# A streaming encoder layer on one core: the feed-forward down projection in two passes over all row blocks, one per half of the output columns

## The reference

```python
x = x + conv_glu_ffn(rms_norm(x, g_ffn), w_up, conv_ffn, b_conv_ffn, w_down)

def conv_glu_ffn(u, w_up, conv_ffn, b_conv_ffn, w_down):
    h = causal_dwconv(u @ w_up, conv_ffn) + b_conv_ffn      # D_FF = 5632, conv width 3
    return (jax.nn.silu(h[..., :D_FF]) * h[..., D_FF:]) @ w_down
```

## Time and profile before

| | |
|---|---|
| median of three runs | 1746.23 us |
| the profiled execution's own time | 1744.13 us |
| its span, first to last instruction | 1742.3 us |
| TensorE busy | 1736.8 us |
| VectorE busy | 1117.4 us |
| ScalarE busy | 938.1 us |
| read from and written to HBM | 326.83 MB, 2.10 MB |
| chunk loads, 512 KB each | 600 |

### The profile page before, as it was taken

The page is one execution under the profiler, slowest core; times in us unless marked ns, Lnnn a source line. Parts: engine busy times, 40 slices in busy tenths (PEclk is TensorE's granted clock), DMA queues, the critical chain, the costliest instruction groups (busy, mean ns, idle before and its releaser), DMA issues.

```text
span 1742.3 us, 26005 instructions
## 1 busy us (share of the span) xinstructions
PE 1736.8 (100%) x8742; PEld 1476.3 (85%) x8742; DVE 1117.4 (64%) x1555; ACT 938.1 (54%) x1273; POOL 9.9 (1%) x22
## 2 busy tenths in 40 slices
PE   9999999999999999999999999999999999999999
PEld 7888888888888888888888888888888888888887
DVE  6788876667855455545665666767777666755554
ACT  7765656667754444444654565555555555544443
POOL 0000000000000000000000000000000000000000
PEclk9999999999999999999999999999999999999999
DMA  8555554476655555556855446555555555655554
GB/s 324 190 172 173 173 171 157 169 166 166 177 184 194 187 193 192 192 188 230 294 183 188 149 159 193 193 193 193 192 185 189 191 187 190 191 193 193 193 193 156
DMA packets 91237, 330.79 MB, mean 190 GB/s; under 512 B 10256, under 2 KB 10512, under 8 KB 90160
## 3 DMA queue, kind: packets, MB, share of 16 engines
q1 hardware_dynamic: 89712, 321.96, 55.7%
q0 software_dynamic: 1472, 8.12, 2.8%
HBM read 326.83 MB, written 2.10 MB: 189 GB/s over the span
## 4 chain that ended last, share of the span: by engine, by line
PE 99%; DMA 0%; DVE 0%; SPq 0%; ACT 0%; issue 0%
PE ps L350 22%; PE ps L331 14%; PE ps L333 14%; PE ps L332 14%; PE ps L353 11%; PE ps L739 4%; PE ps L738 4%; PE ps L737 4%; PE ps L453 1%; PE ps L454 1%; PE ps L452 1%; PE ps L497 1%; PE ps L496 1%; PE ps L609 0%; PE ps L511 0%; PE ps L504 0%
## 5 line engine op out<-in xcount | busy, mean ns | idle before, releaser
L1309 DVE TENSOR_TENSOR w_lo<-w_raw,w_hi 128x1024 fp32r<-128x1024 f32 x598 | 729.4, 1224 | 573.3 <-ACT w_hi L785 572.4
L785 ACT ACTIVATE w_hi<-w_raw 128x1024 fp32r<-128x1024 f32 x598 | 629.0, 1058 | 647.8 <-PE ps L333 310.2
L350 PE MATMUL ps<-u,w_hi 128*128 128x512 f32 x1664 | 580.8, 395 | 0.0
L353 PE MATMUL ps<-u,w_lo 128*128 128x256 f32 x1664 | 461.8, 278 | 0.0
L350 PEld LDWEIGHTS ps<-u,w_hi 128*128 128x128 f32 x1664 | 312.1, 188 | 72.0
L353 PEld LDWEIGHTS ps<-u,w_lo 128*128 128x128 f32 x1664 | 312.7, 188 | 0.2
L331 PE MATMUL ps<-w_hi,u 128*128 128x512 f32 x608 | 240.9, 396 | 0.5 <-DVE w_lo L1341 0.5
L333 PE MATMUL ps<-w_hi,u 128*128 128x512 f32 x608 | 237.2, 390 | 0.0
L332 PE MATMUL ps<-w_lo,u 128*128 128x512 f32 x608 | 237.0, 390 | 0.0
L331 PEld LDWEIGHTS ps<-w_hi,u 128*128 128x128 f32 x608 | 114.4, 188 | 24.4 <-issue 1.1
L333 PEld LDWEIGHTS ps<-w_hi,u 128*128 128x128 f32 x608 | 114.2, 188 | 24.3
(11 more groups left out here) (344 smaller groups left out, 1917.5 us busy)
## 6 DMA issues: line engine op xcount, KB each, us to landing
w_raw<-in_stream SPq DMA_DIRECT2D x600, 512.0 KB, 3.4
x_tok<-in_x SPq DMA_DIRECT2D x2, 1024.0 KB, 8.4
mem_raw<-in_mem_by_feature POOLq DMA_DIRECT2D x2, 1024.0 KB, 9.0
x_tok<-in_x POOLq DMA_DIRECT2D x2, 1024.0 KB, 7.6
mem_tok<-in_mem POOLq DMA_DIRECT2D x2, 1024.0 KB, 14.8
out<-x_tok SPq DMA_DIRECT2D x8, 256.0 KB, 3.3
x_t<-in_x_t SPq DMA_DIRECT2D x7, 256.0 KB, 5.2
w_raw<-in_stream SPq DMA_DIRECT2D x4, 256.0 KB, 4.5
```

Of the source, the lines that this page charges most:

```text
L350: pe.matmul(ps[:, bank + m, :], w_hi[:, s, lo:lo + P], act[:, kc, :, :].rearrange("p h t -> p (h t)"), start=(kc == 0), stop=False)
L353: mm = pe.matmul(ps[:, bank + m, T:2 * T], w_lo[:, s, lo:lo + P], act[:, kc, 0, :], start=False, stop=(kc == KC - 1))
L785: act.activation(w_hi[:, s, :], w_raw[:, s, :], ACT.Copy).then_inc(hi_made, 1)
L1309: TTo(w_lo[:, s, :], w_raw[:, s, :], w_hi[:, s, :].bitcast(F32), ALU.subtract).then_inc(lo_made, 1)
```

## The change

- The 88 chunks of w_down come in another order: first the left 1024 columns for all 44 row blocks, then the right 1024 columns for all 44. TensorE goes over the row blocks twice. A pair of row blocks (`p`, 22 in all) goes with two chunks in each pass.
- Each pair is split once, in pass 0, and stays: the low parts in `h_lo`, in the place of `h_ff`; the high parts in three homes: `h_hi_a` for pairs 0 and 1, `h_hi_b` for pairs 2 to 13 (in the place of most of `u`, the up projection's input), `h_hi_c` for pairs 14 to 21 (in the place of ua, ub, xa, xb and on). `h_st` is gone. `stage` works on a pair (128 by 512) instead of a block (128 by 256); pairs 0 and 1 are staged where round 0 was.
- The loops are gone: all 88 chunks are written out on PE, ACT and DVE.
- PE waits in pass 0 for `h_low` of each pair before the pair's first chunk; ACT and DVE prepare chunks two pairs ahead (`down_split(n + 2)`) and stage pair n + 2 behind that.
- When pass 0 is over, DVE adds banks 0 to 3 in one instruction (128 by 2048) to the left half of `x_tok`, and SyncE's queue stores that half in two transfers of 512 KB behind the last chunk load. At the end PE goes over banks 4 to 7 with the last pair (6 matmuls each), and only these four are added and stored.
- In other parts of the kernel some semaphores are merged into one that counts through them (small_made, small_T, c_tok, mg_parts, norm_mv and so on); each wait is for the same event as before.

```diff
-DOWN_PER = 8
-DOWN_ITER = FC * 2 // DOWN_PER
+QN = FC // 2
...
-        STORES = [(bank, (bank % 4) // 2, (2 * (bank // 4) + bank % 2) * BLK) for bank in range(8)]
+        STORES = [(bank, (bank % 4) // 2, (2 * (bank // 4) + bank % 2) * BLK) for bank in range(4, 8)]
...
@@ SyncE @@
+            sp.wait_ge(sem("half_made"), 1)
+            for t in range(TT):
+                sp.dma_start(out[t * P:(t + 1) * P, 0:1024], x_tok[:, t, 0:1024]).then_inc(sem("stored"), 16)
...
@@ TensorE @@
+            def down_products(s, p, k, t, n, bank, first=False, last=False):
+                rows, at = slice(t * P, (t + 1) * P), slice(n * BLK, (n + 1) * BLK)
+                return three(ps[:, bank, :], h_high(p, k)[:, rows], h_lo[:, 2 * p + k, rows],
+                             w_hi[:, s, at], w_lo[:, s, at], first, last)
+            def down_plain(j, p):
+                g = G_DOWN + 2 * (QN * j + p)
+                for k in range(2):
+                    pe.wait_ge(lo_made, g + k + 1)
                     for t in range(TT):
                         for n in range(2):
+                            mm = down_products((g + k) % SLOTS, p, k, t, n, 4 * j + 2 * t + n, first=(p == 0 and k == 0),
+                                               last=(j == 0 and p == QN - 1 and k == 1))
                     mm.then_inc(w_used, 1)
+            for j in range(2):
+                for p in range(QN):
+                    if j == 0:
+                        if p == 0:
+                            pe.wait_ge(sem("up_sum"), 2 * UP_ITER - 1)
+                        pe.wait_ge(sem("h_low"), p + 1)
+                    elif p == 0:
+                        pe.wait_ge(sem("up_sum"), 2 * UP_ITER)
+                    if j == 0 or p < QN - 1:
+                        down_plain(j, p)
+            for k in range(2):
+                pe.wait_ge(lo_made, G_END - 1 + k)
+            for bank, t, at in STORES:
+                for k in range(2):
+                    mm = down_products((G_END - 2 + k) % SLOTS, QN - 1, k, t, bank % 2, bank, last=(k == 1))
                 mm.then_inc(sem("bank_done"), 1)
...
@@ ScalarE @@
+            def stage(p):
+                act.activation(h_high_pair(p), h_pair(h_ff, p), ACT.Copy).then_inc(sem("h_high"), 1)
+            def down_split(n):
+                g = G_DOWN + 2 * n
+                s = g % SLOTS
+                for k in range(2):
+                    act.wait_ge(landed[s + k], Pos(g + k).landed(0))
+                    act.wait_ge(w_used, g + k - SLOTS + 1)
+                    act.activation(w_hi[:, s + k, :], w_raw[:, s + k, :], ACT.Copy).then_inc(hi_made, 1)
+                    if n == 2 and k == 0:
                         up_first(UP_ITER - 1, 1, xb, ub)
+            for n in range(2 * QN):
+                if n == 0:
+                    up_low(UP_ITER - 1, 1, xb)
+                if n + 2 < 2 * QN:
+                    down_split(n + 2)
+                if n + 2 < QN:
+                    act.wait_ge(w_used, G_DOWN)
+                    act.wait_ge(sem("h_made"), (n + 2) // 2 + 1 if n + 2 < 14 else UP_ITER)
+                    stage(n + 2)
...
@@ VectorE @@
+            def stage(p):
+                dve.wait_ge(sem("h_high"), p + 1)
+                TTo(h_pair(h_lo, p), h_pair(h_ff, p), h_high_pair(p).bitcast(F32), ALU.subtract
+                    ).then_inc(sem("h_low"), 1)
+            def down_split(n):
+                g = G_DOWN + 2 * n
+                s = g % SLOTS
+                for k in range(2):
+                    dve.wait_ge(hi_made, g + k + 1)
+                    TTo(w_lo[:, s + k, :], w_raw[:, s + k, :], w_hi[:, s + k, :].bitcast(F32), ALU.subtract
+                        ).then_inc(lo_made, 1)
+                    if n < 4:
+                        up_end(2 * (n - 2) + k)
+            for n in range(2 * QN):
+                if n == 0:
+                    up_sum(UP_ITER - 1, 1, xb)
+                if n + 2 < 2 * QN:
+                    down_split(n + 2)
+                if n + 2 < QN:
+                    stage(n + 2)
+                if n == QN:
+                    dve.wait_ge(w_used, G_DOWN + 2 * QN)
+                    xs = x_tok[:, :, 0:1024]
+                    TTo(xs, xs, ps[:, 0:4, :].rearrange("p (t n) c -> p t (n c)", t=TT), ALU.add
+                        ).then_inc(sem("half_made"), 1)
```

More of the change, by code:

```diff
@@ L721, in _, with three @@
                 up_pass(Pos(G_UP + UP_PER, j, UP_PER), False)
[L723 to L731, removed]
+            def three(o, a_hi, a_lo, b_hi, b_lo, first, last):
+                pe.matmul(o, a_hi, b_hi, start=first, stop=False)
+                pe.matmul(o, a_hi, b_lo, start=False, stop=False)
+                return pe.matmul(o, a_lo, b_hi, start=False, stop=last)
@@ L732, in down_pass @@
                     for t in range(TT):
-                        a_hi, a_lo = (h_st[:, kc, hl, t * P:(t + 1) * P] for hl in (0, 1))
                         for n in range(2):
[L735 to L739, removed]
@@ L740, in down_pass @@
-                    mm.then_inc(w_used, 1)
[L742 to L761, removed]
-                mm.then_inc(sem("bank_done"), 1)
-                for kc in range(4):
-                    mm = products(7, kc)
-                mm.then_inc(sem("bank_done"), 1)
@@ L1263, in _ @@
             act.wait_ge(sem("h_made"), 1)
-            for kc in range(4):
-                stage(0, kc)
+            stage(0)
+            stage(1)
             with act.Fori(0, UP_ITER - 2) as j:
                 up_pass(Pos(G_UP + 2 * UP_PER, j, UP_PER), j + 2, False)
-            def down_pass(pos, it, last, first=False):
-                for c in range(DOWN_PER):
-                    if first and c == 0:
-                        up_low(UP_ITER - 1, 1, xb)
-                    split(pos, c)
-                    if first and c == 0:
-                        up_first(UP_ITER - 1, 1, xb, ub)
-                    if c >= 4 and not last:
-                        if c == 4:
-                            act.wait_ge(sem("h_made"), it + 2)
-                        act.wait_ge(sem("hst_lo"), 4 * it + (c - 3))
-                        act.wait_ge(w_used, pos.n(c) + 1)
-                        stage(it + 1, c - 4)
-            down_pass(Pos(G_DOWN), 0, False, True)
-            with act.Fori(0, DOWN_ITER - 2) as j:
-                down_pass(Pos(G_DOWN + DOWN_PER, j, DOWN_PER), j + 1, False)
-            down_pass(Pos(G_DOWN + DOWN_PER * (DOWN_ITER - 1)), DOWN_ITER - 1, True)
+            def down_split(n):
[6 more added lines that the diff above has]
+                    if n == 2 and k == 0:
+                        up_first(UP_ITER - 1, 1, xb, ub)
+            for n in range(2 * QN):
[7 more added lines that the diff above has]
+                    stage(n + 2)
         @block.vector
@@ L1906, in up_end @@
                     up_gate(UP_ITER - 1)
-            def down_pass(pos, it, last, first=False):
-                for c in range(DOWN_PER):
-                    if first and c == 0:
-                        up_sum(UP_ITER - 1, 1, xb)
-                    split(pos, c)
-                    if first:
-                        up_end(c)
-                    if c >= 4 and not last:
-                        stage(it + 1, c - 4)
-            down_pass(Pos(G_DOWN), 0, False, True)
-            with dve.Fori(0, DOWN_ITER - 2) as j:
-                down_pass(Pos(G_DOWN + DOWN_PER, j, DOWN_PER), j + 1, False)
-            down_pass(Pos(G_DOWN + DOWN_PER * (DOWN_ITER - 1)), DOWN_ITER - 1, True)
+            def down_split(n):
[19 more added lines that the diff above has]
+                        ).then_inc(sem("half_made"), 1)
             for i, (bank, t, at) in enumerate(STORES):
-                if bank < 4:
-                    dve.wait_ge(w_used, G_END - 4)
-                else:
-                    dve.wait_ge(sem("bank_done"), i - 3)
+                dve.wait_ge(sem("bank_done"), i + 1)
                 xs = x_tok[:, t, at:at + BLK]
```

126 lines of the change are left out of this document (60 added, 66 removed).

## The result

| | before | changed |
|---|---|---|
| median of 19 runs each | 1745.57 us | 1749.24 us |
| range of the runs | 1744.58 to 1747.24 | 1747.20 to 1751.11 |
| profiled execution, its span | 1744.13, 1742.3 | 1748.32, 1746.5 |
| first to last matmul start of the down projection | 239.16 us | 241.54 us |

The ratio is 1.0019, with a 95% interval of 1.0012 to 1.0025: 3.3 us slower (2.1 to 4.4), just inside the 0.2% that I had called no change, though the interval reaches beyond it. The two medians are 3.7 us apart. The forecast was +2.4 us.

What follows compares the result with a forecast made beforehand. TensorE, busy for 1736.8 of 1742.3 us, was taken to bound the kernel. Waits of 2.21 + 0.17 us, all else 0, gave +2.4 us on a 1746.23 us median: 1748.6 us (+0.14%), range 1746.0 to 1751.5.

Steps and rivals of the forecast that it cites:

- TensorE's work: Down projection: 1056 matmuls of the same shape before and after, 239.4 us in both, so 0.
- the merged semaphores: Other parts of the kernel: same events waited for, no instruction moves; 0, bounds 0 to a few tenths.
- the loops: Down projection's loops written out: a jump back costs TensorE nothing, nor does straight code; 0.
- the middle add: DVE's one 128 by 2048 add after pass 0: about 2.6 us, absorbed by spare time; 0.
- the end: Last add and store: same as before for bank 7, bank 6 ends earlier; at most +0.9 us, taken as 0.
- The wait at pair 2: Fifth chunk: TensorE waits for DVE's h_low, restarting at 1512.33 instead of 1510.12; +2.21 us, bounds 1.8 to 2.8.
- The wait at pair 3: Seventh chunk: DVE's stage ends at 1517.79, TensorE wants it at 1517.77; +0.17 us, between 0 and 0.6.
- From pair 4 on: Later pairs in pass 0: staging takes 3.2 of the 5.44 us available per turn; 0.
- The clock: Rival: after the idle gap at pair 2 TensorE goes on at its lower clock, 2.7 us lost, 1751.3 us; chance 0.13.
- Pairs late in every turn: Rival: staging exceeds 5.44 us in each of 18 turns from pair 4; 0.5 over gives 1757.6 us; chance 0.05.
- loops that cost: Rival: nine loop returns each hid a code load of about 1 us, so the change gains, 1739.6 us; chance 0.03.
- No wait at all: Rival: the staging of pair 2 is in time, so the time is 1746.2 us; chance 0.14.

Runs made afterwards that it cites:

- the two partial kernels: Kernel before with only the merged semaphores: 1746.39 us, ratio 1.0003; kernel before with only its looped down-projection rounds written out: 1745.95 us, ratio 1.0002.
- the early staging: Changed kernel with staging of pairs 2 and 3 moved ahead on ScalarE and VectorE, run twice: 1745.39 and 1746.11 us, ratios 0.9998 and 1.0002.
- the two series: Changed kernel, first measured in 19 runs at 1749.24 us (ratio 1.0019), then again unedited in 11 runs at 1748.95 us (ratio 1.0018).
- the changed kernel's second profile: Profile from running the changed kernel again with no edit: 1748.95 us median, ratio 1.0018; down projection length 243.01 us.
- the longer waits: Changed kernel with VectorE's staging of pair 2 moved behind the second up_tap: 1753.79 us, ratio 1.0047; or behind up_gate: 1754.45 us, ratio 1.0052.

## Why the prediction was right, by its steps

- TensorE's work, the merged semaphores, the loops, the middle add, the end: 0 each. Shown by the two partial kernels and above all by the early staging, which leaves all of these in place, has before's length to the last digit and the time of before within 1.2 and 1.9 us. The middle add took 2.28 us (2.6 estimated).
- The wait at pair 2: +2.21 predicted, 2.12 measured, ended by h_lo as named. VectorE's order behind it ran as worked out: 1.82 us later throughout, each start up to pair 3's stage lies within 0.03 us of the predicted one. The stage took 0.68 (0.69 taken). The one number that was off is the time from VectorE's end to TensorE's start: 0.15 taken from the trace's first microseconds, 0.06 here (1513.99 to 1514.05).
- The wait at pair 3: +0.17 predicted, 0.10 measured. It took another form: h_lo was ready at 1519.58, 0.06 ahead of the matmul's start, but behind the time at which the load of the stationary operand would have gone (1519.41), and the late load made the second matmul 0.10 late. The same 0.10 stands behind the first matmul at pair 2, where the sum had no term for it. That the whole, 2.38 us, equals the forecast's 2.38 is luck: 2.12 + 0.10 + 0.10 and 0.06 in small delays, against 2.21 + 0.17.
- From pair 4 on: no gap, as predicted.
- The clock: this was weighed as a rival with 0.13, as if it were one case or the other. It is both: after a wait of 2.1 us the clock fell in 17 of 30 runs. Its price had been 2.7 us; it was 1.5 in the profile and 1.6 to 2.2 between the medians. 2.4 + 0.57 x 1.9 = 3.5 us is what the two series show (3.7 and 3.5 between the medians). So the mechanism of the wait was right and the size of the whole 1 us short: the term that was mis-sized is the clock's, which stood at 0 in the sum and belonged there with about 1.1. The section on what would show it named "starts 0.43 apart behind the gap" as a sign of being wrong. The first profile did not have it; the second did, and so did the majority of the runs.
- The argument against the clock overlooked the end of the trace of before. It said that no wait of 2 us was there to be seen, and that the granted clock was full in all 40 slices. The last matmul starts at 1738.37, and in the same trace the granted clock is:

```profile
1739.00:1740.90 1.90, 0.00 (x0) 0.00 (x0) 0.49 (x1) 0.00 (x0) 0.00 (x0) 1.00 0.29 110
1740.90:1742.30 1.40, 0.00 (x0) 0.00 (x0) 0.00 (x0) 0.00 (x0) 0.00 (x0) 0.50 0.10 38
```

It fell 2.5 us behind that start, and the rest of the span is too short to show in a row of tenths for slices of 43.6 us. The wait forecast at pair 2 was nearly as long from start to start (2.21 + 0.23 us), so the rival deserved more than 0.13.
- The median that the forecast named, 1748.6 us, is 0.6 under the 1749.24 measured, although the change was 1 us larger than forecast. Part of that is luck: the 1746.23 us of before that it was added to, from three runs, was 0.7 above the median of 19. The upper end of the forecast's own range is 0.2 more than its bounds give (1746.23 + 2.8 + 0.6 = 1749.6), unless the tenths allowed to the semaphores are in it.

The sentence quoted from the Trainium skill, that activity releases the throttle ("TensorE: Matmul & The Clock Gate", "What's actually happening"), is borne out here for a wait in the middle of a kernel too: the lower clock follows the wait, and the full clock comes back while TensorE works on (at 1520.1 in the changed kernel's second profile, at 1523.4 and 1524.5 behind the longer waits).
- Pairs late in every turn, and loops that cost: neither was seen. "No wait at all" is what four moved instructions make of the change.

## What to carry to other kernels

When staged operands are wanted at a new pace, look not at the average load of the staging engine but at the first ones that it stages within the new stage: their staging stands in a hand-written order behind whatever that engine still owes to the stage before. Here an engine at 64% load was late there by 2.1 us while it had been idle for 3.1 us just ahead. And where the tensor engine never waits, price a new wait of 2 us with a chance of a slower clock behind it, as a share of the runs and not as an all-or-nothing case. The end of a kernel's own trace, where TensorE has stopped, already shows that the clock can fall that soon.

## What the runs showed of the hardware

- Waits of TensorE in a stream that was dense before, and the lower clock behind them: 1.7 us, in 0 of 11 runs; 2.1 us, in 17 of 30; 4.8 us and 7.1 us, in 5 of 5 each. This goes by each run's mean clock in three digits, which would not show a fall much shorter than the 3.4 us seen. The loss was 1.5 us in the profile with the wait of 2.1, 3.0 and 2.4 with the longer ones. The clock was low for 3.4 us with the wait of 2.1, for 6.8 us with either of the longer ones, and only the part in which TensorE worked cost time.
- With the 2.1 us wait the first matmuls behind it still ran at full pace and the clock fell about 1 us later (1515.73 to 1516.7); with the longer ones it had fallen 0.7 and 2.0 us before TensorE started again.
- Behind the last matmul's start, where TensorE has stopped for good, the granted clock fell after 2.4 to 5.4 us in the twelve profiles.
- When a stationary operand comes just in time for its matmul, its load has lost the 0.22 us by which loads run ahead, and the matmul behind it starts 0.10 us late (pair 3 of the changed kernel).
- Over a thousand matmuls ran at the same pace, 239.16 us from first to last start, with and without a loop around them.
